# A gather moved ahead of the scatters on GpSimd, in the expert loop of a hybrid decoder step

## The reference, cut to what matters

```python
gate = g_w[:, None] * jax.nn.softmax(top_v, axis=-1)          # two experts for each token
...
def expert_block(args):
    xb, e = args
    return (jax.nn.silu(xb @ w_gate[e]) * (xb @ w_up[e])) @ w_down[e]
...
out = jax.ops.segment_sum(ys * row_w[:, None], row_tok, num_segments=T + 1)[:T]
```

## Time and profile before

| | |
|---|---|
| median of 3 runs | 1097.43 us (1094.85 to 1099.52) |
| profiled execution, its time | 1097.43 us |
| its span | 1095.6 us |
| TensorE matmuls busy | 1044.9 us, 95% |
| VectorE busy | 586.5 us, 54% |
| ScalarE busy | 389.9 us, 36% |
| GpSimd busy | 203.6 us, 19% |
| mean granted TensorE clock | 0.989 |

### The profile page before, as it was taken

How to read it: one execution, slowest core, us unless ns; L and a number is a source line. 1 busy time by engine, 2 the same in 40 slices (tenths; PEclk the granted TensorE clock), 3 DMA queues, 4 the chain that set the end, 5 groups by cost and what they waited for, 6 DMA issues and landing times. The chain is left out here.

```text
span 1095.6 us, 29604 instructions
## 1 busy us (share of the span) xinstructions
PE 1044.9 (95%) x12782; PEld 768.3 (70%) x12782; DVE 586.5 (54%) x1166; ACT 389.9 (36%) x776; POOL 203.6 (19%) x191
## 2 busy tenths in 40 slices
PE   8999999999999999999998999999999999999995
PEld 7999999966665549989865755556655555556653
DVE  5336664378875543345626546555555556545552
ACT  6423332166775552213423133133233233133220
POOL 1001200699200000100001221221221221221221
PEclk9999999999999999999999999999999999999998
DMA  7357784000126368676889999999999999999982
GB/s 248 113 164 211 217 275 139 1 14 2 39 65 201 121 232 276 204 262 232 333 315 366 400 395 396 376 402 401 391 387 386 395 394 396 388 391 404 390 332 33
DMA packets 89292, 292.71 MB, mean 267 GB/s; under 512 B 17026, under 2 KB 48450, under 8 KB 63542
## 3 DMA queue, kind: packets, MB, share of 16 engines
q1 hardware_dynamic: 78277, 272.78, 66.9%
q0 software_dynamic: 10752, 17.60, 6.0%
q10 hardware_dynamic: 128, 0.39, 0.1%
HBM read 272.46 MB, written 55.06 MB: 299 GB/s over the span
## 5 line engine op out<-in xcount | busy, mean ns | idle before, releaser
L2914 PE MATMUL bank<-w_all,xeT 128*32 128x256 f32 x6144 | 341.5, 382 | 23.1 <-ACT xeT L1704 22.0
L2914 PEld LDWEIGHTS bank<-w_all,xeT 128*32 128x32 f32 x6144 | 208.8, 111 | 153.5 <-ACT xeT L1704 32.8
L2262 DVE STREAM_TRANSPOSE xeT<-xg 32x256 f32<-32x256 f32 x360 | 156.6, 435 | 124.5 <-DMA xg<-n_scr,tab 119.9
L1704 ACT ACTIVATE xeT<-xeT,gain_p 128x96 f32<-128x96 f32 x240 | 66.9, 361 | 345.9 <-DVE xeT L2262 345.9
L2931 PE MATMUL bank<-w_all,hT 128*32 128x256 f32 x744 | 165.6, 379 | 0.0
L2935 PE MATMUL bank<-w_all,hT 128*32 128x512 f32 x744 | 128.3, 592 | 0.0
L1931 DVE TENSOR_TENSOR_SCAN keep<-keep,unseen 128x1024 f32<-128x1024 f32 (+7 forms) x64 | 94.8, 1514 | 37.8 <-ACT keep L1459 37.8
L2448 PE MATMUL bank<-w_hi,xh 128*128 128x256 f32 x376 | 108.1, 288 | 0.0
L2448 PE MATMUL bank<-w_hi,xl 128*128 128x256 f32 x376 | 105.5, 281 | 0.0
L2448 PE MATMUL bank<-w_lo,xh 128*128 128x256 f32 x376 | 105.5, 280 | 0.0
L1262 POOL DMA_INDIRECT xg<-n_scr,tab x32 | 31.9, 996 | 368.7 <-issue 250.3
(11 more groups left out here) (319 smaller groups left out, 1489.0 us busy)
## 6 DMA issues: line engine op xcount, KB each, us to landing
w_all<-in_w_down SPq DMA_DIRECT2D x64, 1024.0 KB, 24.0
w_all<-in_w_gate SPq DMA_DIRECT2D x64, 1024.0 KB, 22.5
w_all<-in_w_up SPq DMA_DIRECT2D x64, 1024.0 KB, 22.6
k_scr<-in_cache_k SPq DMA_DIRECT2D x32, 256.0 KB, 3.4
v_scr<-in_cache_v SPq DMA_DIRECT2D x32, 256.0 KB, 3.5
pgk<-k_scr SPq DMA_DIRECT2D x32, 256.0 KB, 4.0
w_raw<-in_w_in SPq DMA_DIRECT2D x7, 1024.0 KB, 7.1
pgv<-v_scr SPq DMA_DIRECT2D x4, 1024.0 KB, 6.1
```

The lines of the kernel that those rows point to most:

```text
L1704: last = act.activation(xeT[i][:, k, :], xeT[i][:, k, :], ACT.Copy, scale=gain_p[:, k:k + 1])
L2262: last = dve.transpose(xeT[i][rows_of(s), :, rows_of(g)], lane[:, :, s, :])
L2914: lasts = [pe.matmul(pair_ps(i)[rows_of(q), g, :, :], xeT[i][:, k, rows_of(g)], pair_of(b, i, k, q), start=(k == 0 and g != 1), stop=(k == ...
```

## The change

In the loop over the blocks on GpSimd, gather(b+4) is moved from the end of a turn to its start, ahead of scatter(b) and of moved(b). Its own waits are unchanged: block b+2 must have been read by turn_rows(b+2) and by keep_rows(b+2). No instruction is added or removed.

```diff
             for b in range(NE - 1):
+                if b + 4 < NE:
+                    gather(b + 4)
                 scatter(b)
                 if b < NE - 2:
                     moved(b)
-                if b + 4 < NE:
-                    gather(b + 4)
             pool.wait_ge(s_tab, 1)
```

## The result

| | before | changed |
|---|---|---|
| median | 1097.98 us (1093.66 to 1099.52, 6 runs) | 1103.2 us (1101.19 to 1105.84, 6 runs) |
| ratio, 95% interval | | 1.0057 [1.0031, 1.0085] |
| profiled execution: time, span, clock | 1097.43, 1095.6, 0.989 | 1102.77, 1101.0, 0.993 |

The change makes the kernel about 0.6% slower. The direction was forecast; the size, 1120 us, was not: of the 22.6 us forecast some 5 came. The changed kernel was run on three more chips later; ratios there are 1.0100, 1.0072 and 1.0073. Whether the profile of the kernel before is of the first chip too isn't recorded either.)

What follows compares the result with a forecast made beforehand. TensorE's 15.75 us a block and the weights' 17.3 were taken as floors; the closed ring, 13.3 + 4.44 = 17.74 us a turn, was to add 22.6 us to the 1095.6 us span: 1120 us, range 1094 to 1147.

Steps and rivals of the forecast that it cites:

- The ring: Expert loop: scatter(b-1) issued, its landing, keep_rows(b+2), gather(b+4), scatter(b) issued; forecast 17.74 us a turn against TensorE's 15.75.
- The links, 4.44 us: From both scatters' landing to the next first scatter: wake 0.10, keep_rows 2.18, GpSimd start 0.87, gather issue 0.99, next DMA 0.30.
- L = 13.3: Time from the first scatter's start until both landed: 8.7 (gather's landing) - 1.29 + 5.9; before, about 11.0 us.
- the turn with the wide distance (7.0): Old-order turn shown in the timeline, gather 3.7 us before the scatters; the pair lands 7.0 us behind the gather.
- the close pair's 5.3: Old-order scatters following a gather by only 2.74 us; the pair lands 5.3 us behind the gather, one sample.
- the forecast's sum: Scatter(1) at 604.5 plus 26 turns of 17.74; last gate and up product at 1083.6, 22.6 us later: 1120 us.
- 17.74 us from the first turn: GpSimd's turns from scatter(1) to scatter(27), all 26 taken at 13.3 + 4.44 = 17.74 us.
- Rival (a): Early gather costs the scatters little, or slack hides the late ring: L 12.26 to 12.67, 1092 to 1103 us; chance 0.12.
- Rival (b): Scatters' descriptors don't wait behind the gather's, L below 12.26; TensorE's gains waits vanish: 1092, down to 1089 us; chance 0.10.
- the weights' floor: Weight loads plus gathered and scattered rows at 393 GB/s: 17.3 us a block; caps the gain at 5.5 us.
- Rival (c): Software queue holds the scatters back in full: L = 14.4, 18.8 us a turn, 1150 us; chance within the 0.78 for slower.
- What would show it: Signs to look for in the changed kernel's profile: issue order, scatter landing, waits of keep_rows, VectorE and TensorE, block spacing.

Runs made afterwards that it cites:

- the kernel with both edits: Kernel before with a fourth result buffer and order scatter(b), gather(b+4), moved(b): 1111.1 us, ratio 1.0114 on chip 10.
- Scatter first with the gather set apart: Kernel before with gather(b+4) after scatter(b), ahead of moved(b), also waiting for turn_rows(b+3); three result buffers: 1095.72 us, ratio 0.9981 on chip 13.
- scatter first: Kernel before with gather(b+4) right after scatter(b), ahead of moved(b), three result buffers: 1096.19 us, ratio 0.998 on chip 7; 1092.9 us, 0.9977 on chip 15.
- half a gather: Changed kernel with gathers of blocks 4 to 31 fetching 48 of 96 rows, results wrong: 1082.67 us, ratio 0.9865 on chip 7.

## Why the prediction was right in direction and wrong in size

**The ring exists, and it costs the time.** Shown: with a fourth buffer, which cuts only the link scatter to keep_rows, the changed order goes from ratio 1.0073 to 0.9951 on chip 15 (0.9946 on chip 7), and that buffer alone does nothing for the kernel before (1.0001 on chip 10). The wait moved where the prediction said: from VectorE's gather to keep_rows' scatter.

**The links, 4.44 us.** They hold to the hundredth. From the chain of the changed kernel on chip 15: second scatter landed at 1032.69 + 11.34 = 1044.03, keep_rows at 1044.11 for 2.19, so to 1046.30; the next first scatter is at 1048.47. 1048.47 - 1044.03 = 4.44.

**L = 13.3: the step that failed.** It was mis-sized. L is 1.25 + 11.5 = 12.75 in the median, or 8.8 - 1.29 + 5.2: the gather's landing was right (8.7 forecast), while the pair lands 5.2 behind it (5.3 as the median of the turns), not 5.9. The value 5.9 was a mean drawn toward the turn with the wide distance (7.0); the close pair's 5.3, the row nearest to the new order, would have given 12.7. The turn then is 17.25 us (from 651.62 to 1048.47 in 23 turns), not 17.74. At 27 us for each us of L this half microsecond is most of the miss: with 12.75 and nothing else changed, the forecast's sum gives 1105 us in place of 1120. The place at which L sits makes it so: no change comes out at 12.46 and the forecast's sum at 13.3.

**17.74 us from the first turn: wrong at the start.** The first three turns take 15.52, 16.07 and 17.11 us: L is 9.8, 11.6 and 12.7 there, and only the first still waits for add_rows (1.60 us at 618.44). From the second turn on a turn is L + 4.44, as forecast, but the sum took the late L for the early turns as well.

**The sum again, with what was measured on chip 15.** First scatter at 602.92 in place of 604.5: 1.6 us. Three early turns, 3 x 17.74 - (651.62 - 602.92) = 4.5. The other 23: 23 x 17.74 - (1048.47 - 651.62) = 11.2. From the last scatter to the last product 1065.92 - 1048.47 = 17.45 in place of 17.9: 0.4. Together 17.7, and 1083.6 - 1065.9 = 17.7. What follows the last product is as before: 1100.4 - 1065.9 = 34.5 against 1095.6 - 1061.0 = 34.6. The pieces of one path always add up to its length; what they show is where the miss lies, 11.2 of 17.7 us in the late turns.

**Rival (a)** is close to what came, if only its numbers are read: L between 12.26 and 12.67 and 1092 to 1103 us. On the first chip the mean turn, from the first scatter to the last behind a gather, (603.48 to 1047.63 in 26 turns) is 17.08, which by the links is a mean L of 12.64, and the time is 1103.2 us; on chip 15 L is 12.75 and the time 1104.04. By its mechanism it is the forecast's own, at a smaller L. The fit of the Trainium skill named beside it ("DMA: Bandwidth & Descriptors", section "Anatomy of one DMA — SWDGE (gpsimd) path") would have L at 11.9 (an estimate); the runs disagree, with 12.75 beside the weights' stream. An L of 11.9 lies below 12.26, so by the forecast's own sum it belongs to (b) and not to (a), where the prediction put it. Halving the gather took 1.4 us off L (chip 7 against chip 15). The same fit of the Trainium skill gives 0.5 us for 48 rows of 4 KB (an estimate from that page).

**Rival (b)**, faster, came for the orders with an open ring only, and at the price forecast for it: "5.5 us, 1092" by the weights' floor, measured 1090.8 to 1091.6 with four buffers, 5.6 us under the kernel before on chip 7 and 4.0 to 4.5 on chip 15. **Rival (c)** was nowhere near.

**What would show it.** Gather ahead of scatter by 1.29 us: yes. Second scatter landing after 12.0 us: 11.5. keep_rows waits several us a turn: yes, 178 to 304 us in all. VectorE's wait near nothing: 3.5 us on chips 10 and 13, but 31.9 on the first chip and 65.1 on chip 15, the two where the ring sets the pace: a late ring makes gathers late as well, which I overlooked. TensorE waits absent up to block 8: up to block 12 on chip 15; then about 2 us in every block, some 45 in all: about 1.5 us, 29.4 in 19 places by its row. Blocks every 17.7: 17.25.

**The pauses were not foreseen, and on two chips they set the time.** On chip 15 there are none, and the changed kernel loses as much as on the first chip and on 13 (1.0073 against 1.0057 and 1.0072). So the ring is enough for the loss. On the first chip the chain that ended last runs through the ring too: products there last 11.6 to 12.4 us in blocks 5 to 15 and less behind them, so TensorE's waits for gains hardly show, and the ring catches up with TensorE at block 22.

On chips 10 and 13 it is otherwise. The products last 12.1 to 12.6 us nearly to the end (11.1 in the old order on chip 10), and the chain that ended last runs through them and their pauses, not through the ring. From chip 13, block 29:

```profile
1039.16 9.36 PE bank L2914 x167
1048.52 0.80 issue
1049.32 1.32 PE bank L2914 x19
```

The last product begins there at 1072.62 and 1071.53. From the start of the last keep_rows to the last product it takes 4.35 us where nothing else holds it (chip 15), and by that the ring had let it begin 8.7 and 8.8 us sooner (an estimate). With the ring open, the pauses alone cost 1.1% on chip 10 (the kernel with both edits). So for those two chips the forecast's mechanism, TensorE led by the ring to the end, isn't what the traces show: the ring is closed there, but TensorE is slower still. Without the pauses they should come down to the ring's time and no further (argued, not run).

Two cautions. On chip 13 gains is ready 5.5 to 6 us ahead of its product in each block from 8 to 30; that tells of TensorE's own pace and not of the ring's, since turn_rows, ahead of gains, comes behind add_rows on VectorE, which waits for TensorE (110.9 us in 30 places; chip 15 has 4.4 us in blocks 4 to 8, while its ring falls behind already). The ring does fall behind on chip 13, at 17.15 us a turn against 17.02 a block, too slowly to catch up. And the traces with pauses (first chip, 10 and 13) are also the ones in which the landings of the scatters aren't recorded. Whether the two have to do with one another, and what decides which chip shows pauses, is open.

**Is there a version that beats both?** With four result buffers the changed order was faster than before by about 0.5% on chips 7 and 15, the only ones on which that kernel was tried. Since both edits together lost 1.1% on chip 10, I wouldn't take it as a gain everywhere. Scatter first with the gather set apart was 0.2% faster on chip 13, and is untried elsewhere. Below all of them lie the weights: every kernel with an early gather, an open ring and whole weights waits for them at its end, but for the one with the long pauses.

## What to carry to other kernels

Before an issue is moved ahead of a waiting one on a queue, follow the buffers round: if the moved instruction waits for something that the one behind it releases, a ring closes, and its period (landing plus links) must be compared with the pace of the busiest engine. Where the two are within some per cent, each tenth of a microsecond of a landing counts once for each turn, so take it from the row nearest to the new order rather than a mean toward a farther one, and let the first turns have their slack. Another buffer opens the ring, but it is worth something only as far as the next floor, here the weights' stream. And before one cause is named for a loss, follow the chain that ended last on every chip: here a like loss came by way of the ring on two and by way of slower products on two others.

## What the runs showed of the hardware that I had not expected

- An indirect DMA issued close behind another lands later. With the gather 1.29 us ahead the second scatter lands after 11.5 us, 3.77 us ahead after 10.0, behind the scatters after 9.8; the gather lands after 8.8 us ahead of the scatters and after 11.0 to 11.2 directly behind them. With the weights' bytes halved (223 in place of 394 GB/s) L is about 5.5 in place of 11.0 in the old order (an estimate, see above), and keep_rows never had to wait for a scatter.
- TensorE's weight loads pause while GpSimd issues indirect DMAs, on three chips of five. With two back to back it is one pause of about 0.4 us, 2.4 us after the first one's start (chips 10 and 13); with three it is mostly 1.4 to 1.7 us in all, 1.1 to 3.0 us after the first scatter's start, and 2.3 to 4.4 with the gather last (chip 10). On chip 15 the same kernel shows none; on chip 7 the changed kernel itself wasn't run, but scatter first and half a gather were, without pauses. They show as idle time for "issue" of TensorE's weight loads (28.2 us in 60 places on the first chip). What TensorE lacks there no row shows; a cause was not found.
- The pauses depend on the chip, or on something else that differs between the executions, and where they are long the kernel's time does as well: the two edits together were not run where pauses are absent, but scatter first alone was 0.2% faster on two such chips (7 and 15).
